# A nine-slot weight ring with three experts ahead of the loop, and token rows gathered by indirect DMA, in a two-layer trunk with a mixture of experts

## The chip, the cores and the metric

The kernel runs on one core of one Trainium2 chip, as one launch. The metric is the device time of one execution in microseconds, median of several runs. All data is float32.

## What is computed

Two residual layers over 512 tokens of width 1024 and a final RMSNorm. Layer 0 mixes with a gated linear recurrence beside chunked attention, layer 1 with a gated linear recurrence over eight heads. After each mixer comes a mixture of experts: 32 experts in 4 groups, each token takes the best group and the two best experts in it.

```python
def expert_block(args):
    toks, e = args
    xb = x_pad[toks]
    hb = jax.nn.silu(xb @ w_gate[e]) * (xb @ w_up[e])
    return hb @ w_down[e]
...
h = h + mix
h = h + hier_moe(rms_norm(h, norm_ffn_g[layer]), moe_router_group[layer], moe_router_expert[layer],
                 moe_w_gate[layer], moe_w_up[layer], moe_w_down[layer])
```

Each expert has a gate and an up matrix of 1024x512 and a down matrix of 512x1024, 2 MB each, so 6 MB per expert and 192 MB per layer. 1024 token rows (512 tokens, two experts each) are spread over the 32 experts: 32 rows on average, and the kernel gives each expert a block of CAP = 64.

## The kernel before, in words

Every engine has its own hand-written instruction stream; semaphores order them. `filled[b]` and `drained[b]` count uses of PSUM bank b: TensorE fills, VectorE or ScalarE drains. In the expert loop bank BX (0) holds the transposed token rows, BG (1) gate and up products in its two halves, BH (2) the transposed hidden rows, BY (3) the expert's output, BR (4) the picked token rows.

**Weights.** Two rings of three 2 MB slots, ring_a and ring_b. The mixers use ring_a; their scratch lies partly in ring_b. Experts alternate between the rings: slot 0 gate, slot 1 up, slot 2 down. SyncE issues all weight loads (`expert_load`, L395 to L402): gate and up of expert e+2 wait until the gate/up matmuls of expert e are done, down of e+2 until its down matmuls are. Expert 0 is loaded as soon as ring_b is free of the mixer's scratch, expert 1 only when the mixer's output projection (L490) is over; expert 2 is the first load of the loop.

**Routing.** `route` (VectorE, L1401) makes the one-hot choices, TensorE their running counts (bank "pos", L713 to L717). From these VectorE makes `slots` (L1459, L1461), for every token and expert the place in the expert's block, then the one-hot factors A and B (L1465 to L1469), from which TensorE makes a table of token numbers by place and expert (L726); VectorE turns it into the row numbers `ri` for the scatter (L1482 to L1487).

**Token rows.** For each expert VectorE compares a column of `slots` with a ramp (`select`, L1509): a 128x256 one-hot tile. `pick_rows` (L599) multiplies it with the normalised rows xh: 8 matmuls of 512 columns. ScalarE copies the picked rows out (`picked`, L922), `turn_picked` transposes them (L609), VectorE applies the gain (`turned`, L1521). POOL copies the column for `select` (L1106).

**One expert** on TensorE: `gate_up` (L622, 16 matmuls), `pick_rows` for e+2, `turn_hidden` (L628), `turn_picked` for e+1 (L609), `down` (L636, 8 matmuls). In the trace each float32 matmul stands as two instructions. Meanwhile ScalarE does the silu (L930) and half of the output copy (L936), VectorE the product (L1527), the copy of the hidden rows (L1540) and the other half of the output (L1548); POOL copies the expert's column of `ri` (L1118) and scatters the 64 output rows to DRAM by indirect DMA (L1093), rows without a token being skipped. PE's loop takes two experts per pass; the last two experts pick nothing.

**Around the loop.** After the last scatter ScalarE issues eight loads of the scattered rows (L973) into ring_b; VectorE combines them with h (L1593) and the next norm follows, in layer 1 the final norm (L1602), for which ScalarE has loaded `fin_g` ahead of its waits (L966). SyncE then loads the weights of the layer-1 mixer (L430 to L446): the second of them waits for the combined rows to have been read back. If an expert has more than 64 rows, `more_blocks` does the rest; this doesn't occur in the profiled execution.

## Time and profile before

| what | value |
|---|---|
| runs | 1745.91, 1752.74, 1749.08 us; median 1749.08 us |
| profiled execution, its own time | 1747.05 us |
| its span, first to last instruction | 1745.2 us |
| mean granted clock of TensorE | 0.970 |
| TensorE busy | 1634.0 us (94%) |
| VectorE, ScalarE, POOL busy | 526.9, 369.8, 223.2 us |
| moved by DMA | 463.23 MB, mean 265 GB/s |

All times of rows are microseconds from the span's start unless ns is written. A timeline row gives start, duration, engine, line, operation and tile, and in brackets the idle time before it with what ended it. In the rows of the windows view the PEclk column is the granted clock as a share of full speed. A DMA row ends with the median time from issue to landing. L12 is line 12 of the kernel.

### The profile page before, as it was taken

How to read it: one execution, taken by the hardware profiler on the slowest of the kernel's cores; microseconds unless marked ns; L12 is line 12 of the kernel's file. 1: busy time of each engine (PE TensorE's matmuls, PEld its weight loads, DVE VectorE, ACT ScalarE, POOL GpSimd, SP SyncE). 2: the span in 40 equal slices, each digit the busy share in tenths (PEclk: the TensorE clock that was granted, in tenths of full speed). 3: DMA queues.
4: the chain of work that ended last, by engine and by line, in shares of the span. 5: the costliest groups of instructions: out<-in, count | busy, mean ns of one | idle time of the engine just before them, and what ended most of it. 6: DMA issues, size and time to landing. Idle time of an engine off the chain costs nothing. (4 is left out here: it accounts for less than half of the span.)

```text
span 1745.2 us, 20175 instructions
## 1 busy us (share of the span) xinstructions
PE 1634.0 (94%) x7420; PEld 782.3 (45%) x7420; DVE 526.9 (30%) x1046; ACT 369.8 (21%) x599; POOL 223.2 (13%) x379
## 2 busy tenths in 40 slices
PE   7999997999999999994999999988899999999992
PEld 3444544444444444432577666645333333333330
DVE  4223534321221222224144444433322222222224
ACT  2032421111111111112344445421111111111111
POOL 2000000000000000000144444320000000000000
PEclk9999999999999999996999999999899999999997
DMA  6311033499999999996111112303399999999994
GB/s 217 99 49 54 25 151 145 181 427 429 428 426 428 427 430 428 428 388 245 49 49 49 49 52 99 140 1 145 151 423 428 428 429 429 428 428 428 428 413 168
DMA packets 53953, 463.23 MB, mean 265 GB/s; under 512 B 12800, under 2 KB 12808, under 8 KB 28304
## 3 DMA queue, kind: packets, MB, share of 16 engines
q1 hardware_dynamic: 46336, 445.26, 61.4%
q10 hardware_dynamic: 2448, 8.91, 1.3%
q0 software_dynamic: 5120, 8.40, 1.3%
q8 instruction: 31, 0.51, 0.1%
q14 instruction: 18, 0.15, 0.0%
HBM read 452.03 MB, written 18.89 MB: 270 GB/s over the span
## 5 line engine op out<-in xcount | busy, mean ns | idle before, releaser
L599 PE MATMUL ps<-sb_xh,sb_scr 128*64 128x512 f32 x1024 | 236.7, 602 | 2.4 <-DVE sb_scr L1509 2.4
L622 PE MATMUL ps<-sb_ring_a,sb_scr 128*64 128x512 f32 x1024 | 226.1, 592 | 0.0
L622 PE MATMUL ps<-sb_ring_b,sb_scr 128*64 128x512 f32 x1024 | 225.9, 592 | 0.0
L1527 DVE TENSOR_TENSOR sb_scr<-sb_scr,ps 64x512 f32<-64x512 f32 x64 | 67.6, 1055 | 394.1 <-ACT sb_scr L930 394.1
L755 PE MATMUL ps<-sb_xT,sb_ring_a 128*128 128x512 f32 x384 | 170.4, 598 | 1.1 <-DVE sb_xT L1251 1.1
L1093 POOL DMA_INDIRECT expert_rows<-sb_scr,sb_si x64 | 57.7, 902 | 875.6 <-DVE sb_scr L1548 875.6
L599 PEld LDWEIGHTS ps<-sb_xh,sb_scr 128*64 128x64 f32 x1024 | 86.2, 139 | 137.9 <-issue 137.9
L622 PEld LDWEIGHTS ps<-sb_ring_a,sb_scr 128*64 128x64 f32 x1024 | 88.5, 137 | 131.3 <-issue 131.3
L622 PEld LDWEIGHTS ps<-sb_ring_b,sb_scr 128*64 128x64 f32 x1024 | 83.3, 137 | 135.2 <-issue 135.2
L930 ACT ACTIVATE sb_scr<-ps 64x512 f32<-64x512 f32 x64 | 37.7, 590 | 401.8 <-PE ps L622 401.8
L636 PE MATMUL ps<-sb_ring_a,sb_scr 128*64 128x512 f32 x512 | 118.4, 604 | 1.1 <-issue 1.1
L636 PE MATMUL ps<-sb_ring_b,sb_scr 128*64 128x512 f32 x512 | 116.9, 597 | 0.0
L515 PE MATMUL ps<-sb_xT,sb_ring_a 128*128 128x512 f32 x256 | 110.3, 592 | 1.6 <-DVE sb_xT L1251 1.6
L755 PEld LDWEIGHTS ps<-sb_xT,sb_ring_a 128*128 128x128 f32 x384 | 72.0, 192 | 83.9 <-issue 83.9
L1548 DVE COPY sb_scr<-ps 64x512 f32<-64x512 f32 x64 | 44.4, 693 | 214.0 <-ACT sb_scr L936 214.0
L922 ACT ACTIVATE sb_scr<-ps 128x512 f32<-128x512 f32 x64 | 38.2, 597 | 251.9 <-PE ps L609 226.9
L936 ACT ACTIVATE sb_scr<-ps 64x512 f32<-64x512 f32 x64 | 37.9, 592 | 207.7 <-PE ps L636 207.7
L515 PEld LDWEIGHTS ps<-sb_xT,sb_ring_a 128*128 128x128 f32 x256 | 48.6, 190 | 62.6 <-issue 62.6
L1665 DVE COPY_PREDICATED sb_scr<-sb_masks,ps 128x512 f32<-128x512 uint32 x56 | 40.9, 731 | 104.8 <-PE ps L770 104.8
L770 PEld LDWEIGHTS ps<-sb_scr 128*128 128x128 f32 x512 | 61.2, 192 | 9.1 <-issue 9.1
L636 PEld LDWEIGHTS ps<-sb_ring_b,sb_scr 128*64 128x64 f32 x512 | 40.4, 136 | 55.1 <-issue 55.1
L1540 DVE COPY sb_scr<-ps 128x256 f32<-128x256 f32 x64 | 27.2, 425 | 125.3 <-PE ps L628 125.3
(230 smaller groups left out, 1626.0 us busy)
## 6 DMA issues: line engine op xcount, KB each, us to landing
sb_ring_b<-in_w_gate_dram SPq DMA_DIRECT2D x32, 2048.0 KB
sb_ring_b<-in_w_up_dram SPq DMA_DIRECT2D x32, 2048.0 KB, 17.2
sb_ring_b<-in_w_down_dram SPq DMA_DIRECT2D x32, 2048.0 KB, 14.8
sb_ring_a<-in_w_gate_dram SPq DMA_DIRECT2D x32, 2048.0 KB
sb_ring_a<-in_w_up_dram SPq DMA_DIRECT2D x32, 2048.0 KB, 17.3
sb_ring_a<-in_w_down_dram SPq DMA_DIRECT2D x32, 2048.0 KB, 15.0
sb_ring_a<-in_c_w_in_dram SPq DMA_DIRECT2D x8, 2048.0 KB, 7.8
sb_ring_a<-in_ab_w_in_dram SPq DMA_DIRECT2D x5, 2048.0 KB, 11.3
```

The lines of the kernel that those rows point to most:

```text
L515: mm = nc.tensor.matmul(dst[:], a, b, start=(c == 0), stop=(c == NC - 1))
L599: mm = nc.tensor.matmul(ps[BR][64 * z:64 * z + CAP, :], me["sel"][:, j, t * CAP:(t + 1) * CAP], xh[:, t, z * 512:(z + 1) * 512], start=(t ...
L622: mm = nc.tensor.matmul(ps[BG][64 * s:64 * s + CAP, :], me["xgT"][:, j, c * CAP:(c + 1) * CAP], wblock(r, s, NC)[:, c, :], start=(c == 0), ...
L636: mm = nc.tensor.matmul(ps[BY][64 * z:64 * z + CAP, :], me["hT"][:, c * CAP:(c + 1) * CAP], wblock(r, 2, FC)[:, c, z * 512:(z + 1) * 512], ...
L755: mm = nc.tensor.matmul(dst[:], w[:, c, k, :], xT[:, c, :], start=(c == 0), stop=(c == NC - 1))
L770: mm = nc.tensor.matmul(dst[:, sl], a[:, sl], b[:, sl], start=True, stop=True)
L922: A(me["picked"], ps[BR][:], ACT.Copy).then_inc(drained[BR], 1)
L936: A(me["rows"][0:CAP, 2 + j, 0:512], ps[BY][0:CAP, :], ACT.Copy).then_inc(half_out, 1)
L1093: g.indirect_dma_start(out=y_d[l], out_offset=bass.IndirectOffsetOnAxis(ap=si[j][:, 0:1], axis=0), in_=me["rows"][0:CAP, 2 + j, :], in_off ...
L1527: return v.tensor_tensor(me["hrow"][0:CAP, :].rearrange("p (c q) -> p q c", c=FC), by_q(me["silu"][64:128, j, :]), by_q(ps[BG][64:128, :]) ...
L1548: v.tensor_copy(me["rows"][0:CAP, 2 + j, 512:1024], ps[BY][64:128, :]).then_inc(drained[BY], 1)
L1665: drains(v.copy_predicated(dst, masks[:, L - 1, :].bitcast(U32).unsqueeze(1).broadcast_to([P, NT, P]), src), job)
```

## The change

It does three things. (1) The six slots of the two rings become one ring of nine; an expert's three matrices go to slots by expert number modulo 3. The room comes from `xh` (it is now slot 8) and from the scratch, part of which now lies in slots 6 and 7. Experts 0 to 2 are loaded ahead of the loop: expert 1 without the wait for the output projection, expert 2's gate and up as the projection frees slots 2 and 0, its down when xh has been transposed and stored. In layer 1 expert 0 is loaded during the mixer. Loads of expert e+3 wait for expert e. (2) The normalised rows are stored to DRAM (ScalarE issues four DMAs) and POOL gathers the 64 rows of an expert with an indirect DMA, two experts ahead; eight transposes of 64x128 (`turn_in`) bring them to BX. `select`, `pick_rows`, `picked`, `turn_picked`, `slots` and bank BR go. The table is completed (one more column of steps, and `xi`) before the first gather. (3) PE's loop takes six experts per pass, the load of `fin_g` is issued after the last scatter's wait, and the second and third weight load of the layer-1 mixer no longer wait for the rows read back.

```diff
+SLOTS, SLOT = 9, 8 * 512
+EXPERT_SLOTS = ((3, 4, 5), (6, 7, 1), (2, 0, 8))
...
+        yrows = slots(3, 2).rearrange("p (a d) -> p a d", d=D)
...
+            def weight_load(l, e, q, part):
+
+                w, s = (w_gate, w_up, w_down)[part], EXPERT_SLOTS[q][part]
+                sp.dma_start(ring[:, s, :], by_partition(w[l, bass.ds(e, 1)])).then_inc(ring_in[s], 16)
+
+            def expert_load(l, e, q):
+
+                sp.wait_ge(filled[BG], e + (moe_base[l][BG] - 2))
+                weight_load(l, e, q, 0)
+                weight_load(l, e, q, 1)
+                sp.wait_ge(filled[BY], e + (moe_base[l][BY] - 2))
+                weight_load(l, e, q, 2)
...
+                else:
+                    wait_full(sp, ("c", HEADS_C - 1, 3))
+                    sp.wait_ge(y_ready, HEADS_C)
+                if l == 0:
+                    for part in range(3):
+                        weight_load(l, 0, 0, part)
+                for part in range(3):
+                    weight_load(l, 1, 1, part)
+                for part in range(2):
+                    wait_full(sp, ("out", l, NT - 1, part))
+                    weight_load(l, 2, 2, part)
+                wait_full(sp, ("xt", 2 * l + 1, NT - 1, 1))
+                sp.wait_ge(xh_stored[l], 16 * NT)
+                weight_load(l, 2, 2, 2)
+                with sp.Fori(1, NE // 3) as i:
+                    for q in range(3):
+                        expert_load(l, i * 3 + q, q)
...
-            sp.wait_ge(filled[BG], moe_base[0][BG] + NE)
+            sp.wait_ge(filled[BG], moe_base[0][BG] + NE - 2)
...
                 if i == 1:
-                    sp.wait_ge(yrow_in[NT - 1], 32)
-                if i == 2:
                     sp.wait_ge(filled[BY], moe_base[0][BY] + NE)
...
+                if i == 3:
+                    sp.wait_ge(h_ready, 2 * NT)
+                    for part in range(3):
+                        weight_load(1, 0, 0, part)
...
-                if ahead >= 2:
-                    pick_rows(l, e + 2, j)
+                gate_up(three, q % 2).then_inc(filled[BG], 1)
+                if not last:
+                    turn_gathered(l, e + 1, i * 3 + (q + 1) // 2, (q + 1) % 2)
                 pe.wait_ge(drained[BG], e + (base[BG] + 1))
...
-                if ahead >= 1:
-                    turn_picked(l, e + 1)
...
-                pick_rows(l, 0, 0)
-                turn_picked(l, 0)
-                pick_rows(l, 1, 1)
...
+                turn_gathered(l, 0, 0, 0)
+                for e in range(6):
+                    expert(l, e, 0, e)
+                with pe.Fori(1, NE // 6) as i:
+                    for q in range(6):
+                        expert(l, i * 6 + q, i, q)
...
                 norm(2 * l + 1)
+                for t in range(NT):
+                    act.wait_ge(xh_ready, (2 * l + 1) * NT + t + 1)
+                    act.dma_start(xg_d[l][t * P:(t + 1) * P, :], xh[:, t, :]).then_inc(xh_stored[l], 16)
...
+            def gather_rows(l, j):
+                pool.sem_inc(moving, 1)
+                g.indirect_dma_start(out=me["gat"][0:CAP, j, :], out_offset=None, in_=xg_d[l],
+                                     in_offset=bass.IndirectOffsetOnAxis(ap=gi[j][:, 0:1], axis=0),
+                                     bounds_check=T - 1, oob_is_err=False).then_inc(gathered[j], 16)
...
                     if ahead:
-                        pool.wait_ge(sel_ready, e + (l * NE + 2))
-                        slots_of(e + 3, 1 - j)
+                        pool.wait_ge(filled[BX], e + (base[BX] + 1))
+                        fetch(e + 2, j)
...
+                    if ahead:
+                        pool.wait_ge(idx_copied, e * 2 + (2 * l * NE + 4))
+                        gather_rows(l, j)
...
+                st.then(v.tensor_scalar(tab[:, 2, :], tab[:, 0, :], T + 0.5, -float(T), ALU.is_gt, ALU.mult))
+                v.tensor_copy(ri[:], tab[:, 1, :])
+                v.tensor_tensor(xi[:], tab[:, 1, :], tab[:, 2, :], ALU.add).then_inc(table_ready, 1)
+                turned(l, 0, 0)
```

## Rows read from the trace of the kernel before

**Rows 1.** The page: bytes moved, in 40 slices of the span.
```profile
GB/s 217 99 49 54 25 151 145 181 427 429 428 426 428 427 430 428 428 388 245 49 49 49 49 52 99 140 1 145 151 423 428 428 429 429 428 428 428 428 413 168
```

**Rows 2.** Windows, in the loop of layer 1 (columns: page's engines, PEclk, DMA share, GB/s).
```profile
1400.00:1500.00 100.00, 100.00 (x488) 38.93 (x488) 21.35 (x34) 11.87 (x20) 8.53 (x21) 1.00 1.01 428
```

**Rows 3.** Timeline of TensorE, one expert of the loop in layer 0.
```profile
499.68 7.07 PE L622 MATMUL ps<-sb_ring_b,sb_scr 128*64 128x512 f32 x32
506.54 3.63 PE L599 MATMUL ps<-sb_xh,sb_scr 128*64 128x512 f32 x16
510.50 0.66 PE L609 MATMUL ps<-sb_ident,sb_scr 128*128 128x128 f32 x4
511.13 3.65 PE L636 MATMUL ps<-sb_ring_b,sb_scr 128*64 128x512 f32 x16
514.59 7.07 PE L622 MATMUL ps<-sb_ring_a,sb_scr 128*64 128x512 f32 x32
```

**Rows 4.** DMA issues, up matrix: experts 2, 31 of layer 0, then of layer 1.
```profile
sb_ring_b<-in_w_up_dram SPq DMA_DIRECT2D x1, 2048.0 KB, 13.3
...
sb_ring_a<-in_w_up_dram SPq DMA_DIRECT2D x1, 2048.0 KB, 19.3
...
sb_ring_b<-in_w_up_dram SPq DMA_DIRECT2D x1, 2048.0 KB, 12.1
...
sb_ring_a<-in_w_up_dram SPq DMA_DIRECT2D x1, 2048.0 KB, 20.2
```

**Rows 5.** The page, DMA queues: packets, MB, share; this is all 64 scatters.
```profile
q0 software_dynamic: 5120, 8.40, 1.3%
```

**Rows 6.** Timeline of TensorE, experts 30 and 31; last row layer 1.
```profile
768.03 7.07 PE L622 MATMUL ps<-sb_ring_b,sb_scr 128*64 128x512 f32 x32
...
781.36 7.07 PE L622 MATMUL ps<-sb_ring_a,sb_scr 128*64 128x512 f32 x32
...
791.25 5.09 PE L636 MATMUL ps<-sb_ring_a,sb_scr 128*64 128x512 f32 x16 [0.56 <-issue]
...
1710.60 3.65 PE L636 MATMUL ps<-sb_ring_a,sb_scr 128*64 128x512 f32 x16 [0.56 <-issue]
```

**Rows 7.** Timeline, from the normalised rows to the loop; last two rows layer 1.
```profile
287.55 1.33 DVE L1240 TENSOR_SCALAR sb_xh<-sb_h,sb_rstd 128x1024 f32<-128x1024 f32 x1
...
308.82 0.29 DVE L1459 SCALAR_TENSOR_TENSOR sb_scr<-ps,sb_scr 128x128 f32<-128x128 f32 x1 [1.29 <-PE ps L717]
...
309.98 5.09 PE L599 MATMUL ps<-sb_xh,sb_scr 128*64 128x512 f32 x16 [1.20 <-DVE sb_scr L1509]
310.08 0.28 DVE L1465 TENSOR_TENSOR sb_scr<-ps,sb_scr 128x128 f32<-128x128 f32 x1
...
312.48 0.42 DVE L1469 TENSOR_TENSOR sb_scr<-sb_iota,sb_scr 128x256 f32<-128x256 f32 x1
...
320.79 7.06 PE L622 MATMUL ps<-sb_ring_b,sb_scr 128*64 128x512 f32 x31
...
320.99 0.18 DVE L1482 COPY sb_scr<-ps 64x32 f32<-64x32 f32 x1 [3.79 <-PE ps L726]
...
321.63 0.17 DVE L1487 CAST sb_ri<-sb_scr 64x32 uint32<-64x32 f32 x1
...
1228.43 6.66 PE L599 MATMUL ps<-sb_xh,sb_scr 128*64 128x512 f32 x16 [1.20 <-DVE sb_scr L1509]
...
1240.81 7.06 PE L622 MATMUL ps<-sb_ring_b,sb_scr 128*64 128x512 f32 x31
```

**Rows 8.** The scatter's line L1093, all 64 of them.
```profile
DMA to landing us min/median/max: 2.5/7.9/8.7
```

**Rows 9.** Timeline, from the last scatter of layer 0 to the read back.
```profile
798.54 0.89 POOL L1093 DMA_INDIRECT expert_rows<-sb_scr,sb_si  x1 [13.68 <-DVE sb_scr L1548]
802.30 4.80 ACTq L973 DMA_DIRECT2D sb_ring_b<-expert_rows  x8
```

**Rows 10.** Windows, at the end of layer 0's loop.
```profile
788.00:792.00 4.00, 1.61 (x9) 0.64 (x8) 1.45 (x2) 0.59 (x1) 0.00 (x0) 0.85 0.68 197
```

More of the change, by code:

```diff
@@ new lines, in trunk @@
+        m1.update(carve(high, [("f", (T,)), ("eb", (T,)), ("qe", (2, T)), ("dl", (3, P)), ("kh", (3, P)),
+                               ("st", (2, 3 * P)), ("sq", (T,)), ("rs", (T,))]))
+        m1.update(carve(slots(8, 1), [("y", (8, T))]))
+        me = carve(low, [("gat", (2, D)), ("rows", (2, D))])
+        me.update(carve(high, [("xgT", (2, NC * CAP)), ("hT", (FC * CAP,)), ("silu", (F,)),
+                               ("hrow", (F,)), ("lg", (NT, NG + NE)), ("em", (NT, NE)), ("key", (NT, NE)),
+                               ("M0", (NT, NE)), ("M1", (NT, NE)), ("M", (NT, NE)), ("pos", (2, NT)),
+                               ("A", (2, NT, CAP)), ("B", (2, NT, NE)), ("g4", (NT, NG)), ("goh", (NT, NG)),
+                               ("ex", (NT, 5)), ("tab", (3, NE)), ("w", (12, NT)), ("lgT", (T,)), ("Msum", (NT, NE))]))
@@ L174, in trunk @@
+        me.update(carve(high, [("fin_g", (D,))]))
+        yrows = slots(3, 2).rearrange("p (a d) -> p a d", d=D)
         filled = [sem(f"filled{b}") for b in range(8)]
         drained = [sem(f"drained{b}") for b in range(8)]
-        ring_in = {(r, s): sem(f"ring_in_{r}{s}") for r in "ab" for s in range(3)}
+        ring_in = [sem(f"ring_in{s}") for s in range(SLOTS)]
         x_in = [sem(f"x_in{t}") for t in range(NT)]
@@ L213, in trunk @@
         xh_stored = [sem(f"xh_stored{l}") for l in range(2)]
-        col_ready, sel_ready = sem("col_ready"), sem("sel_ready")
+        gathered = [sem(f"gathered{j}") for j in range(2)]
         scattered = [sem(f"scattered{j}") for j in range(2)]
@@ L246, in plan_moe @@
             moe_base.append(list(bk.uses))
-            for b in (BX, BG, BH, BY, BR):
+            for b in (BX, BG, BH, BY):
                 bk.uses[b] += NE
@@ L407, in moe_loads @@
                     wait_full(sp, ("O", NA - 1))
-                expert_load(l, 0, 0, True)
-                for nb in range(2):
-                    wait_full(sp, ("out", l, NT - 1, nb))
-                expert_load(l, 1, 1, True)
-                with sp.Fori(0, NE // 2 - 1) as i:
-                    expert_load(l, i * 2 + 2, 0, False)
-                    expert_load(l, i * 2 + 3, 1, False)
+                else:
[15 more added lines that the diff above has]
+                        expert_load(l, i * 3 + q, q)
+                for e in range(NE // 3 * 3, NE):
+                    expert_load(l, e, e % 3)
             def more_loads(l):
@@ L630, in turn_hidden, with down @@
                 return mm
-            def down(r):
+            def down(slots):
                 for c in range(FC):
@@ L728, in moe @@
                 fills(mm, ("tab", l))
-                expert(l, 0, 0, 0)
-                with pe.Fori(0, NE // 2 - 2) as i:
-                    expert(l, i * 2 + 1, i, 1)
-                    expert(l, i * 2 + 2, i + 1, 0)
-                expert(l, NE - 3, NE // 2 - 2, 1)
-                expert(l, NE - 2, NE // 2 - 1, 0, ahead=1)
-                expert(l, NE - 1, NE // 2 - 1, 1, ahead=0)
+                turn_gathered(l, 0, 0, 0)
[4 more added lines that the diff above has]
+                        expert(l, i * 6 + q, i, q)
+                for e in range(NE // 6 * 6, NE):
+                    expert(l, e, NE // 6, e % 6, last=e == NE - 1)
                 more_blocks(l)
@@ L1457, in route @@
                 wait_full(dve, job)
-                st.then(v.scalar_tensor_tensor(out=me["slots"], in0=bank(job)[:, 0:NT * NE].rearrange(
-                    "p (t n) -> p t n", t=NT), scalar=1.0, in1=M, op0=ALU.add, op1=ALU.mult))
-                st.then(v.tensor_scalar(me["slots"], me["slots"], -1.0, None, ALU.add))
-                for e in range(2):
-                    select(l, e, e)
                 for k, Mk in ((0, M0), (1, M1)):
```

290 lines of the change are left out of this document (111 added, 179 removed).

## The prediction

> **What bounds the kernel now.** First I read the bytes by slices [rows 1]: twice there are about ten slices at 427 to 430 GB/s, the expert loops, and between them long stretches at 50 to 150. The windows view of such a stretch [rows 2] shows DMA at a share of 1.01 and TensorE busy for 100 of 100 us: both are full, and the question is which of them sets the pace. The timeline [rows 3] says TensorE: experts follow each other at 514.59 - 499.68 = 14.91 us without a gap, gate/up 6.86, picking 3.6, turns about 1.0, down 3.46. The landings [rows 4] say how near DMA is. Loads are issued at TensorE's pace, yet issue to landing of the up matrix grows from 13.3 to 19.3 us over 29 experts in layer 0 and from 12.1 to 20.2 in layer 1: 0.21 and 0.28 us each. So DMA's own pace is 15.12 to 15.19, I take **15.15 us per expert**, and it is slower than TensorE; only the lead from two preloaded experts hides it. TensorE's loop can get faster by its lead only: what counts is how many bytes are left to move once the loop starts, and at what rate.
>
> **The change, part by part.**
>
> *Picking goes, turning comes.* Per expert 3.6 us of matmuls [rows 3] leave TensorE, and the turn of picked rows (0.66). Eight transposes of gathered rows come, about 0.9 us (estimate from the four of L609). They don't add: the last experts of layer 0 already run without picking [rows 6], at 781.36 - 768.03 = 13.33 us, and there TensorE waits between gate/up and down for silu and product (788.43 to 791.25, 2.82 us); the transposes fall into that wait. So TensorE needs **13.34 us per expert**, 1.8 below DMA. DMA becomes the bound.
>
> *Gathers on the DMA engines.* The same 16 engines now also read the token rows. All 64 scatters, 8.40 MB, took 1.3% of the engines' span, so 22.7 us or 0.355 us each [rows 5]; a gather moves the same rows the other way, so I take 0.35 and DMA's pace becomes **15.50 us**. Bounds: below, nothing (reads might fit beside the writes, though a share of 1.01 speaks against it); above, 0.71, if the empty half of the 64 places or an uneven spread over the engines costs as much again. I take the scatter's row, as it is the nearest.
>
> *Three experts ahead.* 29 instead of 30 experts remain for the loop. Expert 2 fits into the idle time before it: the output projections and the routing lie there, and the slices stand at 145 GB/s [rows 1]. The four stores of the normalised rows (2 MB, 5 us at 428 GB/s) start behind the last norm step at 287.55 + 1.33 and are needed only when the table is done, past 314: hidden by the routing. Expert 0 of layer 1 goes into the mixer's stretch at 49 to 99 GB/s: hidden.
>
> *Sum for the loop.* Up of expert 3 lands 0.7 us (issue of gate ahead of it, estimate) plus 12.1 to 13.3 [rows 4], so 13.4 us, after gate/up of expert 0. Up of expert 31 lands 28 x 15.50 = 434.0 us later, then gate/up 7.07, wait 2.82, down 3.65: the loop ends 461.0 us after gate/up of expert 0. Before it was 796.34 - 327.85 = 468.5 in layer 0 and 1714.25 - 1247.87 = 466.4 in layer 1 [rows 6, 7]. Gain 7.5 and 5.4 us. Early in the loop TensorE works off the lead and no load waits for it: at 13.34 against 15.50 it is out of lead near expert 14.
>
> *Start of the loop.* Now the first expert needs the table. From the running counts at 308.82 [rows 7]: `slots` and two selections go (310.08 - 308.82 = 1.26 saved), so the factors are ready at 312.90 - 1.26 = 311.64; table matmuls 1.0 to 2 us, take 1.5; the table steps 0.81 and two more at 0.21 each, with the wake-up 1.35; table ready near 314.5. POOL then copies an index (0.3) and gathers. For the gather of an idle queue the scatter gives 2.5 us from issue to landing, and up to 3.76 from the last scatter's issue to the read back [rows 8, 9]: take 3.1, so 318. Turning 1.2, gain 0.85, and gate/up starts near 320.1, where it started at 320.79. But picking no longer warms TensorE up. The first picks took 5.09 and 6.66 us where the later ones took 3.63 [rows 3, 7], so 1.5 to 3.0 us go onto gate/up now: take 2.2. It ends 1.5 us later than before in layer 0, and by the same steps 0 us later in layer 1, whose picks had been colder. Bounds -3 to +5 us per layer.
> By the Trainium skill (DMA: Bandwidth & Descriptors, Anatomy of one DMA) a DMA issued by POOL takes about 2.0 us plus its bytes at 436 GB/s, an estimate of 2.3 us here; by that the start would come 0.8 us earlier per layer than by the row I use.
>
> *Between the layers.* Two mixer loads of 2 MB (9.8 us at 428 GB/s) are now issued right behind the last down matmuls, ahead of the last scatter and the read back. In an idle queue the scatter was done in 3.76 us [rows 9]; in a full one it lands after 7.9 [rows 8]. So the read back comes 0 to 6 us later, take 3.5. Nothing is won by the earlier loads, as the mixer's first weights are there anyway. POOL: its gather stands ahead of the scatter of expert e and behind that of e-1, and it has a period and a half to land in; 7.9 us fits.
>
> *At the end.* `fin_g` is issued ahead of the eight read-backs, 0.6 us by their 4.80 for eight [rows 9], and 0.5 MB of transfer: +1.2 us.
>
> *Total.* Layer 0: -7.5 + 1.5 + 3.5 = -2.5; layer 1: -5.4 + 0 + 1.2 = -4.2. Together **-6.7 us** on a profiled execution of 1747.05 (span 1745.2). The median of the runs shown is 2.0 us above it, so the forecast is 1749.08 - 6.7, about **1742 us**. This case has its own range of 1733 to 1752.
>
> **The rivals.**
>
> (a) *The gathers cost DMA nothing.* Then 57 x 0.35 = 20 us more are won: 1722. For it speaks that scatters write to DRAM and gathers read from it; against it the share of 1.01, as weight loads are reads too. Chance 0.08.
>
> (b) *A gather costs twice the scatter's share* (0.71 each): 20 us more, 1762, slower than before. It decides from 0.47 us per gather on, where the 6.7 us are eaten. For it: 5120 packets are 80 for each 64 places, half of which are empty (8.40 MB are 2050 rows of 4 KB), and the engine with most rows sets the landing. Chance 0.15.
>
> (c) *The clock.* TensorE will wait for weights in every expert (15.50 - 13.34 = 2.2 us) besides the waits around the turns. In layer 0's last expert, which had such waits, the granted clock fell to 0.85 of full speed over four microseconds, so to its lower level of 1.2 GHz for part of it, and down took 5.09 instead of 3.65 [rows 6, 10]; in layer 1 the same expert kept the full 2.4 GHz level. One such fall costs 1.4 to 3.0 us of TensorE; it decides where more than 2.2 us per expert are lost. At 3.0 each time it would be 57 x 0.8 = 46 us: 1788, and with half the experts about 1765. It checks itself: a TensorE that has become the bound no longer waits for weights. Chance 0.12.
> The Trainium skill (TensorE: Matmul & The Clock Gate, HAM oscillation) says that a DMA wait before each group of matmuls throws the engine back to 1.2 GHz every time, which speaks against this change; this trace agrees in one of two last experts.
>
> (d) *The third expert isn't ahead.* Its down waits for the stores and the transposes; if anything of it slips behind the loop's start, the lead is two and a part, up to 15.5 us lost per layer: 1773 at worst. For it speaks only the chain of waits in SyncE; the idle slices speak against. Chance 0.04.
>
> **How the numbers follow.** The main case has 0.61. A measurement of this kernel tells about 0.5%, 8.7 us, from no change, and the forecast lies at -7: of the main case 0.43 is faster by more, 0.55 within, 0.02 slower. Faster: 0.26 + 0.08 from (a) = 0.34, rounded to 0.35. Slower: (b) mostly, (c), (d) and a little of the main case, 0.30. Within: 0.35. The range of 1722 to 1772 takes in (a), (b), (d) but for its end, and the milder half of (c); it leaves out about 0.15.
>
> **What would show it.** In the profile of the changed kernel: DMA at a share of 1.0 through both loops, and a TensorE that waits about 2 us before gate/up from the middle of each loop on, its busy share there below 90%. Issue to landing of up near 38 us late in the loop, and experts following at 15.4 to 15.6 us: more says (b) when TensorE waits for DMA, (c) when it doesn't and L622 takes over 7.07. The software queue should hold 2 x 8.4 MB at 2.6%. First gate/up at 320 in layer 0; the gather behind the table landing in 2.5 to 3.8 us. Read back of layer 0 about 9 us behind the last down matmuls, where it was 6. The forecast is wrong if the period is under 15.2 or over 15.9, or if the loop is still paced by TensorE.

## The result, and the profile after

The changed kernel takes 1796.69 us (median of 4 runs, 1793.12 to 1797.92), the kernel before 1748.99 us beside it. The ratio is 1.0268, 95% interval 1.0243 to 1.0293: 47.7 us slower, where 1742 us with a range up to 1772 was forecast. The profiled executions have spans of 1791.1 and 1745.2 us; the trace below has to explain 45.9 us.

The page of the changed kernel: TensorE's busy line, the bytes by slices, the two main queues, and the two gate/up and turn groups.

```profile
PE 1474.3 (82%) x6652; PEld 710.0 (40%) x6652; DVE 502.7 (28%) x982; ACT 331.9 (19%) x535; POOL 287.0 (16%) x447
...
GB/s 211 96 47 53 30 255 214 257 397 408 414 409 410 411 411 401 405 384 195 134 102 48 48 94 48 1 188 141 244 405 399 406 412 412 414 405 408 411 342 159
...
q1 hardware_dynamic: 46336, 445.26, 61.9%
q0 software_dynamic: 10240, 16.80, 2.8%
...
L616 PE MATMUL ps<-sb_ring,sb_work 128*64 128x512 f32 x2048 | 471.2, 613 | 71.8 <-DMA sb_ring<-in_w_up_dram 59.4
...
L622 PE MATMUL ps<-sb_ident,sb_work 64*128 64x64 f32 x256 | 27.6, 228 | 83.4 <-DVE sb_work L1498 83.4
...
sb_ring<-in_w_up_dram SPq DMA_DIRECT2D x64, 2048.0 KB, 39.5
```

The slices are the news. Where the kernel before moved 426 to 430 GB/s in nearly all full slices of its loops [rows 1], this one moves 397 to 414, though it has the gathered rows to move besides the weights. The queue of the indirect DMAs, q0, doubled its bytes, as forecast, and has a share of 2.8%, where 2.6% was forecast from [rows 5]. TensorE now waits 59.4 us in all for the up matrix.

Windows of the changed kernel: the stretch of [rows 2], then the whole of each loop (us, busy time and count of PE, PEld, DVE, ACT, POOL, then PEclk, DMA share, GB/s).

```profile
1400.00:1500.00 100.00, 76.25 (x370) 28.69 (x368) 17.69 (x25) 7.68 (x13) 13.84 (x25) 0.96 1.01 410
...
330.00:800.00 470.00, 373.95 (x1828) 146.98 (x1828) 87.09 (x123) 35.96 (x61) 64.52 (x118) 0.96 1.00 407
1272.00:1740.00 468.00, 379.25 (x1811) 146.06 (x1812) 87.11 (x123) 35.47 (x61) 64.55 (x118) 0.94 1.00 405
```

The DMA share is 1.00 to 1.01 as before, so the engines are as occupied, but 5% fewer bytes pass. The timeline of TensorE in the middle of layer 0's loop answers to [rows 3]:

```profile
603.64 7.09 PE L616 MATMUL ps<-sb_ring,sb_work 128*64 128x512 f32 x32 [0.68 <-DMA sb_ring<-in_w_up_dram]
610.65 0.71 PE L608 MATMUL ps<-sb_ident,sb_work 64*128 64x64 f32 x8
612.55 0.43 PE L622 MATMUL ps<-sb_ident,sb_work 64*128 64x64 f32 x4 [1.19 <-DVE sb_work L1498]
613.55 3.65 PE L630 MATMUL ps<-sb_ring,sb_work 128*64 128x512 f32 x16 [0.56 <-issue]
620.01 7.09 PE L616 MATMUL ps<-sb_ring,sb_work 128*64 128x512 f32 x32 [2.82 <-DMA sb_ring<-in_w_up_dram]
```

One expert takes 620.01 - 603.64 = 16.37 us. TensorE is through with it at 613.55 + 3.65 = 617.20, so after 13.56 us, and the wait of 2.82 us ahead of the next gate/up is for the up matrix, so for the DMA.

The start of both loops and the end of layer 0, on the timeline, answer to [rows 7, 9] (in the second part the read back is split by the listing, the row shows six of its eight issues):

```profile
313.67 0.18 DVE L1474 TENSOR_TENSOR sb_xi<-sb_work 64x32 uint32<-64x32 f32 x1
...
315.08 1.14 POOL L1083 DMA_INDIRECT sb_work<-norm_rows,sb_gi  x1 [0.99 <-POOL sb_gi L1094]
...
318.77 1.09 PE L608 MATMUL ps<-sb_ident,sb_work 64*128 64x64 f32 x8 [6.08 <-DMA sb_work<-norm_rows,sb_gi]
...
320.64 9.22 PE L616 MATMUL ps<-sb_ring,sb_work 128*64 128x512 f32 x32 [0.78 <-DVE sb_work L1485]
...
815.17 0.80 SPq L453 DMA_DIRECT2D sb_ring<-in_c_w_in_dram  x2
...
817.34 0.90 POOL L1077 DMA_INDIRECT expert_rows<-sb_work,sb_si  x1 [13.63 <-DVE sb_work L1517]
826.88 3.73 ACTq L957 DMA_DIRECT2D sb_ring<-expert_rows  x6
...
1261.60 9.77 PE L616 MATMUL ps<-sb_ring,sb_work 128*64 128x512 f32 x32 [0.78 <-DVE sb_work L1485]
```

The first gate/up starts at 320.64 and takes 9.22 us, where a later one takes 7.09: TensorE had waited for the gather, and in the trace its granted clock is 0.5, the lower of its two levels, until 325.0. In layer 1 the first takes 9.77, with the lower level until 1267.1. Below, such a start is called cold. From the scatter to the read back pass 9.54 us where 3.76 passed before.

Laid side by side (us; "loop" is from the start of the first gate/up to the end of the last down matmul):

| part | before | after | difference |
|---|---|---|---|
| to the first gate/up of layer 0 | 320.7 | 320.6 | 0 |
| loop of layer 0 | 475.7 | 494.5 | +18.8 |
| from it to the first gate/up of layer 1 | 444.4 | 446.4 | +2.0 |
| loop of layer 1 | 473.6 | 494.9 | +21.3 |
| from it to the end | 30.9 | 34.6 | +3.7 |

All but 6 us lies in the loops. The weights' packets say in what form: the trace records each of the 16 KB packets of the weight queue. Worked out from these records, in layer 0 from 420 to 700 us:

```
kernel before     mean 0.614 us
changed kernel    mean 0.639 us, 5% of them 0.818 or more
```

The slow ones, of 0.7 us or more, come in one group for each gather, most of them 2.4 to 3.4 us long and the longest 5.1, with up to 16 slow packets at once, as many as there are DMA engines. Weight packets that overlap only a gather's rows took 0.760 us on average; those beside a scatter's rows in the kernel before took 0.613. So the scatters' rows don't do this.

The rows' own packets are the smaller part. The share of q0 is 2.8% of 1791.1 us, or 50.2 us, and the scatters took 22.7 of it before [rows 5]: 27.5 us for 64 gathers, 0.43 us each.

### The profile page after: what moved, and what is told of

The parts are those of the page before. It is cut to its first block and busy times, and to the rows that moved or that the text cites. A ratio compares the mean times of both kernels' runs of the same rounds, so it can differ in the third digit from the quotient of the medians.

```text
span 1791.1 us, 18344 instructions
## 1 busy us (share of the span) xinstructions
PE 1474.3 (82%) x6652; PEld 710.0 (40%) x6652; DVE 502.7 (28%) x982; ACT 331.9 (19%) x535; POOL 287.0 (16%) x447
## 5 line engine op out<-in xcount | busy, mean ns | idle before, releaser
L616 PE MATMUL ps<-sb_ring,sb_work 128*64 128x512 f32 x2048 | 471.2, 613 | 71.8 <-DMA sb_ring<-in_w_up_dram 59.4
L616 PEld LDWEIGHTS ps<-sb_ring,sb_work 128*64 128x64 f32 x2048 | 164.6, 141 | 372.9 <-issue 337.3
L630 PE MATMUL ps<-sb_ring,sb_work 128*64 128x512 f32 x1024 | 265.9, 666 | 35.9 <-issue 33.8
L1498 DVE TENSOR_TENSOR sb_work<-sb_work,ps 64x512 f32<-64x512 f32 x64 | 65.4, 1023 | 493.6 <-ACT sb_work L919 493.6
L1077 POOL DMA_INDIRECT expert_rows<-sb_work,sb_si x64 | 58.8, 919 | 810.5 <-DVE sb_work L1517 810.5
L752 PE MATMUL ps<-sb_work,sb_ring 128*128 128x512 f32 x384 | 168.5, 592 | 1.1 <-DVE sb_work L1242 1.1
L630 PEld LDWEIGHTS ps<-sb_ring,sb_work 128*64 128x64 f32 x1024 | 88.5, 152 | 165.3 <-issue 162.7
L919 ACT ACTIVATE sb_work<-ps 64x512 f32<-64x512 f32 x64 | 37.8, 590 | 524.8 <-PE ps L616 524.8
L923 ACT ACTIVATE sb_work<-ps 64x512 f32<-64x512 f32 x64 | 37.9, 592 | 414.6 <-PE ps L630 414.6
L530 PE MATMUL ps<-sb_work,sb_ring 128*128 128x512 f32 x256 | 110.3, 592 | 1.6 <-DVE sb_work L1242 1.6
L752 PEld LDWEIGHTS ps<-sb_work,sb_ring 128*128 128x128 f32 x384 | 71.3, 190 | 82.6 <-issue 82.6
L530 PEld LDWEIGHTS ps<-sb_work,sb_ring 128*128 128x128 f32 x256 | 48.6, 190 | 62.6 <-issue 62.6
L1083 POOL DMA_INDIRECT sb_work<-norm_rows,sb_gi x64 | 61.3, 958 | 54.5 <-POOL sb_si L1105 48.3
L767 PEld LDWEIGHTS ps<-sb_ring 128*128 128x128 f32 x512 | 61.2, 192 | 9.1 <-issue 9.1
L767 PE MATMUL ps<-sb_ring 128*128 128x128 f32 x512 | 62.4, 275 | 0.0
## 6 DMA issues: line engine op xcount, KB each, us to landing
sb_ring<-in_w_gate_dram SPq DMA_DIRECT2D x64, 2048.0 KB, 34.6
```

The source lines that it names most:

```text
L530: mm = nc.tensor.matmul(dst[:], a, b, start=(c == 0), stop=(c == NC - 1))
L616: mm = nc.tensor.matmul(ps[BG][64 * z:64 * z + CAP, :], me["xgT"][:, j, c * CAP:(c + 1) * CAP], wblock(slots[z], NC)[:, c, :], start=(c == ...
L630: mm = nc.tensor.matmul(ps[BY][64 * z:64 * z + CAP, :], me["hT"][:, c * CAP:(c + 1) * CAP], wblock(slots[2], FC)[:, c, z * 512:(z + 1) * 512],
L752: mm = nc.tensor.matmul(dst[:], w[:, c, k, :], xT[:, c, :], start=(c == 0), stop=(c == NC - 1))
L767: mm = nc.tensor.matmul(dst[:, sl], a[:, sl], b[:, sl], start=True, stop=True)
L1077: g.indirect_dma_start(out=y_d[l], out_offset=bass.IndirectOffsetOnAxis(ap=si[j][:, 0:1], axis=0), in_=me["rows"][0:CAP, j, :], in_offset= ...
```

## The experiments

The theory: something about the gather makes the weights beside it slower. The rivals: nine slots in flight do it by themselves; the falls of TensorE's clock do it.

**1. No gathers in the loop**, and three kernels in which a plain DMA of 32 fixed rows on the same queue stands for the gather. These, and the other kernels with a plain copy below, leave out the choice of rows. Where a kernel writes partitions above 63, it also clears the whole buffer ahead of the loop; this edit isn't shown.

```diff
 # e1_none
-                        gather_rows(l, j)
-                pe.wait_ge(gathered[j], k * 16 + 16 * (l * (NE // 2) + 1))
+                pe.wait_ge(gathered[j], 16 * (l + 1))
 # e2_plain, in place of the indirect gather
+                g.dma_start(me["gat"][0:32, j, :], xg_d[l][0:32, :]).then_inc(gathered[j], 16)
 # e3_spread
+                g.dma_start(me["gat"][:, j, 0:256], xg_d[l][0:32, :].rearrange("r (q n) -> (r q) n", q=4)
+                            ).then_inc(gathered[j], 16)
 # e4_dram
+                g.dma_start(dump[j], xg_d[l][0:32, :]).then_inc(gathered[j], 16)
```

> This kernel leaves out the gathers of experts 2 to 31 of each layer: those experts compute on the rows gathered for experts 0 and 1. Everything else of the changed kernel stays (nine slots, three experts ahead, the scatters, the copies of the indices). Theory G (the gather costs the DMA engines about 1.0 us per expert: 0.4 for its own rows and 0.6 because the weight packets beside it take 0.64 us in place of 0.61): the late experts of both loops come down from 16.25 to 16.5 us each to about 15.2, mean weight packets to 0.61 us, and with 29 experts in each layer the time is 1797 - 58 x 1.0 = 1738 us. Rival D (the deeper backlog of loads makes the weight packets slower by itself): packets stay at 0.64 us, only the rows' own 0.4 us goes, about 1773 us. Rival C (the falls of TensorE's clock, not the DMA, set the pace): the falls of 3.4 us stay and the time stays within 8 us of 1797.

> This kernel leaves out the choice of rows: in place of each indirect gather it copies the first 32 rows of the layer's normed tokens, in one plain DMA on the same queue, to the first 32 partitions. Same bytes, about the same rows per packet, same partitions written; no dummies and no scattered reads. Theory P (the place written, a few partitions, is what slows the weights' packets): still 1790 to 1800 us. Rival I (indirection or the scattered reads do it): 1740 to 1765 us, weight packets at 0.61 us.

> As the kernel with the plain copy, the same 32 rows and 128 KB, but written as 1 KB pieces over all 128 partitions. Theory P (few partitions are the cause): 1750 to 1770 us, with weight packets back at about 0.61 us and only the bytes' own time left. Rival I or rival H (reading the rows from DRAM is the cost, wherever they go): no more than 5 us from the plain copy to 32 partitions.

> As the kernel with the plain copy, but the 32 rows go to a scratch in DRAM and not to the SBUF; TensorE turns rows that stay zero. It leaves out the rows altogether and keeps their reads, the queue, and the bytes. Theory P (the write into the SBUF is what slows the weights): 1745 to 1765 us, weight packets about 0.61 us. Rival H (the read from DRAM beside the weights' reads is the cost): as slow as the plain copy to 32 partitions or slower, near 1790 us.

Measured: without gathers 1725.23 us (ratio to before 0.9866, interval 0.9845 to 0.9887). Plain copy to partitions 0 to 31: 1781.65 us (1.0190, 1.0172 to 1.0209). The same bytes over all partitions: 1744.03 us (0.9971, 0.9959 to 0.9984). From DRAM to DRAM: 1742.65 us (0.9968, 0.9954 to 0.9982). All four came out below the ranges that were expected of the theory; e2_plain lies between its two theories' ranges, nearer to the first. The windows view, 1400 to 1500 us, of the four in this order:

```profile
1400.00:1500.00 100.00, 85.48 (x428) 33.78 (x426) 20.51 (x29) 8.28 (x15) 8.41 (x21) 0.97 1.01 429
```
```profile
1400.00:1500.00 100.00, 81.04 (x380) 30.53 (x378) 16.98 (x24) 7.08 (x12) 12.49 (x28) 0.93 1.01 409
```
```profile
1400.00:1500.00 100.00, 83.74 (x408) 32.18 (x404) 19.13 (x27) 7.67 (x13) 12.42 (x28) 0.95 1.01 426
```
```profile
1400.00:1500.00 100.00, 83.83 (x410) 32.33 (x408) 19.81 (x28) 8.26 (x14) 12.60 (x28) 0.95 1.01 428
```

429, 409, 426, 428 GB/s. A backlog of nine slots costs nothing: e1_none has it at 429. Indirection and scattered reads aren't the main cost, since a plain copy of 32 neighbouring rows moves as few bytes as the gather (409 against 410). They, or something else that the plain copy leaves out, may hold a part of the 15 us by which e2_plain is faster than the changed kernel; 6.8 us of these lie in the two loops. Reading the rows isn't the cost either, since the copy to DRAM reads them as well. It is the write into partitions 0 to 31.

Without gathers the experts follow each other at the pace of the weights alone, in layer 0 of e1_none (755.56 - 664.61) / 6 = 15.16 us:

```profile
664.61 7.09 PE L616 MATMUL ps<-sb_ring,sb_work 128*64 128x512 f32 x32 [1.62 <-DMA sb_ring<-in_w_up_dram]
...
755.56 7.09 PE L616 MATMUL ps<-sb_ring,sb_work 128*64 128x512 f32 x32 [1.78 <-DMA sb_ring<-in_w_up_dram]
```

Its loops took 460.5 and 460.0 us, which prices everything that follows: a gather costs (loop - 460.5 or 460.0) / 29, as 29 experts' weights are loaded in a loop. For the changed kernel that is **1.17 and 1.20 us**, where the forecast had 0.35.

**2. Which partitions?** Three more plain copies and, in c1_half, the real rows, gathered as half rows by 128 indices.

```diff
 # e7_every4
+                g.dma_start(me["gat"][0:P:4, j, :], xg_d[l][0:32, :]).then_inc(gathered[j], 16)
 # e8_half2
+                g.dma_start(me["gat"][0:P:2, j, 0:512], xg_d[l][0:32, :].rearrange("r (q n) -> (r q) n", q=2)
+                            ).then_inc(gathered[j], 16)
 # e5_sbuf
+                g.dma_start(me["gat"][0:32, j, :], me["gat"][32:64, j, :]).then_inc(gathered[j], 16)
 # c1_half; the table is made for both halves, an index is 2 * token + half
+                g.indirect_dma_start(out=me["gat"][:, j, 0:512], out_offset=None,
+                                     in_=xg_d[l].rearrange("t (z n) -> (t z) n", z=2),
...
```

> Plain copy of 32 whole rows (4 KB each) as in the kernel that took 1781.65 us, but to every fourth partition (0, 4, ... 124) in place of partitions 0 to 31. It leaves out the choice of rows. The copy in 1 KB pieces to all partitions took 1744.03 us. Theory N (what slows the weights is that the rows' destinations are neighbours, and so share the same ports into the SBUF): within 6 us of 1744. Rival L (what slows them is that a whole 4 KB row goes to one partition, wherever that lies): within 6 us of 1782.

> Plain copy of the same 32 rows as 64 half rows of 2 KB to every second partition. It leaves out the choice of rows. Theory N: within 6 us of 1744, since the destinations lie over the whole SBUF. Rival L: about halfway, 1755 to 1770 us.

> Plain copy of 32 rows of 4 KB from partitions 32 to 63 of the SBUF to partitions 0 to 31: nothing is read from DRAM. It leaves out the rows altogether. If the write to neighbouring partitions is all of the extra price: 1775 to 1790 us, as the copy from DRAM (1781.65). If the DRAM read has a part in it: less, 1745 to 1770 us. If reading neighbouring partitions costs as much as writing them: above 1800 us.

> The changed kernel with the right rows, but gathered by 128 indices as half rows of 2 KB: the first halves to partitions 0 to 63, the second halves to partitions 64 to 127 (an expert's rows fill the first half of each), turned by four transposes of 128 x 128 in place of eight of 64 rows. Theory N: the conflict is over twice as many partitions, so the extra of 38 us (1781.65 - 1744.03) is halved or better: 1750 to 1775 us. Rival I (that part of the changed kernel's 1797 us which the plain copy to the same partitions does not have, 15 us, is the price of indirection, and doubles with twice the indices): 1785 us or more.

Measured: 1740.21 us (every fourth partition), 1740.86 (half rows, every second), 1779.80 (from the SBUF, nothing read from DRAM), 1755.61 us with the right rows (c1_half; ratio to before 1.0037, 1.0024 to 1.0050). All four lie in the ranges expected of theory N. Rival L falls: a whole row may go to one partition. The copy within the SBUF settles that the write alone is slow, and that reading 32 neighbouring partitions beside it adds nothing. And c1_half is the first version with the real rows near the old time.

**3. The same with the real rows.** An expert's rows fill the first places of its block of 64, so renumbering the places moves them. c2_iota does only this to the changed kernel, c3_spread to c1_half. c4_both also restores the old wait ahead of the second mixer load.

```diff
-            g.iota(iota[:], [[1, CAP]], base=0,
+            g.iota(iota[:], [[1, CAP // 2], [CAP // 2, 2]], base=0,
...
 # c4_both, in the loads of the layer-1 mixer, i == 1
                     sp.wait_ge(filled[BY], moe_base[0][BY] + NE)
+                    sp.wait_ge(yrow_in[NT - 1], 32)
```

> The changed kernel with one line changed: the places of an expert's 64 slots are numbered 0, 32, 1, 33, ..., so that its first 32 rows (nearly all that it has) are gathered to partitions 0, 2, ... 62 in place of 0 to 31. Same rows, bytes, packets and instructions. Theory N (neighbouring destinations share ports): as with half rows to two halves of the SBUF, twice as many places: 1750 to 1770 us. Rival (only the number of instructions and descriptors of the indirect gather counts): 1790 to 1800 us.

> The kernel with half rows on 128 indices (1755.61 us) with the same renumbering of the slots: the 64 half rows of an expert go to every second partition, as in the plain copy that took 1740.86 us. Theory N: 1737 to 1747 us, the whole extra price gone, weight packets at 0.617 us or less. Rival I (indirection itself costs what is left between 1740.86 and 1755.61): 1750 us or more.

> The kernel with the spread half rows, and the second weight load of the next layer's mixer waits for the read back of the expert rows, as it did in the kernel before. Theory B (the three weight loads that now go out ahead of the last scatter and the read back delay these by some 6 us): 3 to 6 us less than the kernel with the spread half rows alone. Rival (those loads are needed by the first projections, and then start them later): within 2 us of it, or slower.

Measured: c2_iota 1789.02 us, a miss for theory N (1750 to 1770): rows on 0, 2, ... 62 are hardly faster than on 0 to 31. c3_spread 1746.66 us (0.9986, 0.9977 to 0.9995): 50 us of the changed kernel's time are gone. It differs from that kernel by half rows, 128 indices and other transposes as well; the plain copies of whole rows, e2_plain and e7_every4, differ by the partitions alone (and the clearing), and they are 41 us apart. c4_both 1742.53 us (0.9963, 0.9949 to 0.9977), 4.1 us less again. The windows view of c2_iota, then of c3_spread:

```profile
1400.00:1500.00 100.00, 78.80 (x376) 29.36 (x374) 17.69 (x25) 7.68 (x13) 13.11 (x24) 0.95 1.01 408
```
```profile
1400.00:1500.00 100.00, 82.26 (x382) 30.91 (x380) 19.83 (x28) 8.26 (x14) 14.40 (x26) 0.97 1.01 426
```

c2_iota (32 places among 0 to 62: 408 GB/s) against c1_half (0 to 31 and 64 to 95: 426) says that neighbours are not the point, and points to the halves of the SBUF. On the wait, the timeline of c3_spread and then of c4_both:

```profile
794.01 0.80 SPq L454 DMA_DIRECT2D sb_ring<-in_c_w_in_dram  x2
796.18 0.91 POOL L1083 DMA_INDIRECT expert_rows<-sb_work,sb_si  x1 [12.11 <-DVE sb_work L1530]
805.96 3.85 ACTq L963 DMA_DIRECT2D sb_ring<-expert_rows  x8
```
```profile
792.37 0.91 POOL L1084 DMA_INDIRECT expert_rows<-sb_work,sb_si  x1 [12.11 <-DVE sb_work L1531]
796.16 3.86 ACTq L964 DMA_DIRECT2D sb_ring<-expert_rows  x8
...
808.90 0.80 SPq L455 DMA_DIRECT2D sb_ring<-in_c_w_in_dram  x2
```

Two mixer loads ahead of the scatter make it land 9.78 us behind its issue, and 3.79 us without them. The stretch between the loops shrank from 447.2 to 440.5 us.

**4. One half or neighbours, tested alone.**

```diff
 # f1_twohalves
+                for z in range(2):
+                    g.dma_start(me["gat"][64 * z:64 * z + 16, j, :], xg_d[l][16 * z:16 * z + 16, :]
+                                ).then_inc(gathered[j], 16)
 # f2_lower
+                g.dma_start(me["gat"][0:64:2, j, :], xg_d[l][0:32, :]).then_inc(gathered[j], 16)
 # g1_upper
+                g.dma_start(me["gat"][64:P:2, j, :], xg_d[l][0:32, :]).then_inc(gathered[j], 16)
```

> Plain copy of 32 whole rows in two DMAs of 16 rows, to partitions 0 to 15 and 64 to 79; it leaves out the choice of rows. Theory S (the two halves of the SBUF, partitions 0 to 63 and 64 to 127, have paths of their own, and rows that all go to one half are what slows the weights' packets): 1738 to 1750 us and weight packets of 0.61 to 0.62 us, though the destinations are neighbours. Rival N (neighbouring destinations, in whichever half): 1765 us or more.

> Plain copy of 32 whole rows in one DMA to partitions 0, 2, ... 62; it leaves out the choice of rows. Theory S: as slow as the copy to partitions 0 to 31 (1781.65 us), within 8 us, since all rows go to the lower half. Rival N: about halfway to the kernel with every fourth partition (1740.21), 1755 to 1765 us or less.

> Plain copy of 32 whole rows in one DMA to partitions 64, 66, ... 126; it leaves out the choice of rows. Theory S, mended after the run with two DMAs (rows slow the weights' packets while all rows in flight at one time go to one half of the SBUF; of those two DMAs one follows the other): as slow as the copy to 0, 2, ... 62 (1781.93 us), within 8 us. Rival L (only the lower partitions are slow): within 6 us of 1740. Rival M (what counts is the number of partitions in any half): the same forecast as S, so it is not told apart here.

Measured: 1781.93 us for 0, 2, ... 62 and 1785.69 for 64, 66, ... 126, both as theory S has it, so the one half is as slow as the other when all rows go to it. But 1809.84 us for 0 to 15 and 64 to 79, the slowest of all placements, at 399 GB/s:

```profile
1400.00:1500.00 100.00, 78.49 (x368) 29.34 (x364) 17.00 (x24) 7.08 (x12) 13.55 (x30) 0.93 1.01 399
```

For this run theory S, as it was put, fails: both halves were written, and it was slow. Its two DMAs follow each other: in the trace their rows stand in two bursts of 16, for one expert from 522.6 and from 524.4 us. So at any one time the rows go to 16 neighbouring partitions of one half. That it is this, and not having two DMAs for each expert, which makes it the slowest wasn't tried alone; what the second DMA adds to the queue's records are 1024 packets of 4 bytes. Together the placements give this table (each price is worked out from the two loops as above; packets are the means of the weight queue's 16 KB packets, 420 to 700 us):

| kernel | partitions that an expert's rows reach | price of one gather or copy, us | weight packet, us |
|---|---|---|---|
| e1_none | no gathers | 0 (it sets the zero) | 0.614 |
| e4_dram | none | 0.28, 0.32 | 0.614 |
| e7_every4 | 0, 4, ... 124 | 0.31, 0.30 | 0.614 |
| e8_half2 | 0, 2, ... 126 | 0.38, 0.32 | 0.615 |
| e3_spread | all | 0.38, 0.39 | 0.617 |
| c3_spread | 0, 2, ... 126 | 0.32, 0.37 | 0.616 |
| c1_half | 0 to 31, 64 to 95 | 0.49, 0.52 | 0.616 |
| e5_sbuf | 0 to 31 | 0.97, 1.00 | 0.640 |
| f2_lower | 0, 2, ... 62 | 1.03, 1.02 | 0.642 |
| g1_upper | 64, 66, ... 126 | 1.11, 1.00 | 0.644 |
| e2_plain | 0 to 31 | 1.08, 1.06 | 0.641 |
| c2_iota | 0, 2, ... 62 | 1.01, 1.10 | 0.641 |
| changed kernel | 0 to 31 | 1.17, 1.20 | 0.639 |
| f1_twohalves | 0 to 15, then 64 to 79 | 1.42, 1.58 | 0.655 |

The Trainium skill (SBUF — State Buffer, Door 1: The DMA port swizzle) has a rule that fits every line: bits 4 to 2 and bit 6 of the partition number choose one of 16 ports for the DMA side, so that partitions 0 to 63 reach eight of them and adding 32 changes nothing. By it the rows that cost 0.3 to 0.5 us reach all 16 ports (or none), those at about 1.0 to 1.2 reach eight, and f1_twohalves four at a time. The runs agree in order and grouping; they don't show the ports themselves.

Left open is why c1_half costs 0.15 us more than c3_spread per gather and the changed kernel 0.1 more than c2_iota. In c1_half more packets of the queue carry only empty places (598 packets of 8 bytes from 420 to 700 us, against 117 in c3_spread), so some engines may have more rows than others; this wasn't tried alone. It can't be told of the other pair, whose packets have the same sizes and numbers.

**5. TensorE's clock.** In the loops of c4_both the granted clock falls to its lower level for a while in 10 of each loop's groups of gate/up or down matmuls, besides the cold first one, as it does in 12 and 15 of them in the changed kernel; the kernel before kept 1.00 up to the last expert [rows 2, 10]. The fillers are matmuls on constants into the bank that picking no longer uses.

```diff
+            def fill(n):
+                for _ in range(n):
+                    nc.tensor.matmul(ps[4][0:CAP, :], ones[:, 0:CAP], keep[:], start=True, stop=True)
 # c5_fill: 8 behind down.  f3_fill: 1 behind turn_gathered, 2 behind down.
 # f4_warm: 3 ahead of the turn of expert 0.  g2_fill: those 3, then 1 behind turn_gathered, 1 behind down.
```

> The kernel with the spread half rows and the wait, and eight matmuls of 512 columns per expert on constants into an unused bank, issued behind the down projection: what TensorE did for picking before, about 1.6 us. They fill its waits for the weights. Theory F (the DMA sets the pace, and the falls of the clock cost only where TensorE ends last): granted clock up to 0.96 or more, time within 4 us of the kernel without them. Rival C (the falls of the clock are paid in the time): 10 us or more faster. Rival (the filled stretches make TensorE the bound again): slower by 5 us or more.

> The kernel with the spread half rows and the wait (1742.53 us), and three matmuls of 512 columns per expert on constants into an unused bank: one where TensorE waits for the activation (1.3 us idle there) and two behind the down projection, 0.88 us each. TensorE then needs about 13.34 + 1.8 = 15.1 us per expert, under the DMA's 15.5. Theory F (the DMA sets the pace; the falls of the clock are paid at the ends of the loops only): granted clock up from 0.946 to 0.97 or more, time within 5 us of 1742.5. Rival C (the falls are paid all along): 10 us or more faster. Rival (the filling takes back what was gained): over 5 us slower.

> The kernel with the spread half rows and the wait, and three matmuls on constants in the 6 us in which TensorE waits for the first gather of each layer. In the profile of the kernel without them the first gate and up projection takes 9.3 us, at half clock in part, against 7.1 later. Theory W (it starts slow because TensorE stood idle before it, and the loop's end moves with its start): about 2 us less in each layer, 1736 to 1741 us. Rival (the DMA sets the loop's end whatever the first expert takes): within 1.5 us of 1742.5.

> The fastest kernel so far (1735.54 us: spread half rows, the wait, three matmuls on constants ahead of the first expert) and per expert two such matmuls, one in the wait for the activation and one behind the down projection. With three, TensorE needed 15.2 us per expert in the trace and was the bound over all 32 experts (32 x 15.2 = 486 against the DMA's 468 for 29). With two it needs about 14.3 us, 32 x 14.3 = 458, under the DMA's 468. Theory F (the falls of the clock are no part of the time where the DMA sets the pace): 1732 to 1738 us, with the clock at full speed in the loops. Rival C (the falls are paid): 1730 us or less. Rival (any filling is paid): 1745 us or more.

c5_fill took 2106.65 us. I had sized the filler by the 3.6 us that picking took for as many instructions, but picking wrote its two output halves in turn; here the eight matmuls, all into one half, take about 7 us. f3_fill, sized by the mean of one, still lost: 1772.89 us (1.0133), where at most 5 us more than c4_both's 1742.53 were expected. Its timeline shows an expert of 523.73 - 508.42 = 15.31 us:

```profile
508.42 7.40 PE L622 MATMUL ps<-sb_ring,sb_work 128*64 128x512 f32 x31
515.76 0.66 PE L647 MATMUL ps<-sb_ident,sb_work 128*128 128x128 f32 x4
516.34 1.07 PE L616 MATMUL ps<-sb_keep,sb_ones 128*64 128x512 f32 x2
517.94 0.43 PE L628 MATMUL ps<-sb_ident,sb_work 64*128 64x64 f32 x4 [0.52 <-DVE sb_work L1518]
518.93 3.65 PE L636 MATMUL ps<-sb_ring,sb_work 128*64 128x512 f32 x16 [0.56 <-issue]
...
523.73 7.40 PE L622 MATMUL ps<-sb_ring,sb_work 128*64 128x512 f32 x31
```

That is below the DMA's 15.5 and yet too much, as the two don't count the same experts: TensorE does 32 of them (this one took 15.31, the next 15.05; 32 x 15.2 = 486, the loops took 485.2 and 485.3), the DMA moves 29. The point where they are equal is 470 / 32 = 14.7 us.

f4_warm took **1735.54 us** (0.9926, 0.9912 to 0.9939; 1736 to 1741 expected), g2_fill 1734.26 (0.9921, 0.9908 to 0.9935). Timeline of c4_both's first gate/up, then f4_warm's:

```profile
320.02 9.31 PE L618 MATMUL ps<-sb_ring,sb_work 128*64 128x512 f32 x32 [0.78 <-DVE sb_work L1506]
```
```profile
321.20 7.09 PE L622 MATMUL ps<-sb_ring,sb_work 128*64 128x512 f32 x32 [0.78 <-DVE sb_work L1511]
```

Its first gate/up is as fast as the later ones from the start, and the loops end 2.2 and 2.6 us sooner after their start. That is 4.8 us of the 7.0 between the medians; the runs of c4_both alone lie 8 us apart, so the rest isn't told from that spread. Windows of the loops of f4_warm, then of g2_fill:

```profile
330.00:780.00 450.00, 376.36 (x1722) 145.83 (x1724) 86.81 (x124) 35.95 (x61) 67.56 (x120) 0.96 1.01 425
1250.00:1690.00 440.00, 366.45 (x1678) 140.14 (x1676) 84.96 (x120) 35.35 (x60) 65.69 (x116) 0.96 1.00 424
```
```profile
330.00:780.00 450.00, 412.09 (x1842) 156.08 (x1842) 88.03 (x124) 36.38 (x62) 67.56 (x120) 1.00 1.01 425
1250.00:1690.00 440.00, 403.34 (x1800) 150.94 (x1799) 85.19 (x120) 35.35 (x60) 66.71 (x119) 1.00 1.01 425
```

With the granted clock at 1.00 throughout, g2_fill's loops take 467.9 and 467.9 us, and f4_warm's, at 0.96, 467.9 and 467.9. The falls inside a loop that the DMA paces cost nothing. The cold first expert cost its 2.2 and 2.6 us, as the loads of the loop wait for the first gate/up to be done. In the changed kernel itself this wasn't tried.

## Why the prediction was wrong

- **The step that failed** is "Gathers on the DMA engines": "a gather moves the same rows the other way, so I take 0.35", with an upper bound of 0.71. The scatter's row [rows 5] priced the bytes, and for the bytes it was right: 0.28 to 0.39 us where the rows are spread evenly over both halves or stay in DRAM. It could not price the other direction. A scatter reads partitions 0 to 31, a gather writes them, and the write costs 1.17 to 1.20 us, over the bound, because the weights' own packets slow down meanwhile: 0.760 us beside its rows where 0.614 is the mean without gathers. That is a cost to other transfers, and the prediction had no term for it. The excess of 0.83 us on 58 gathers is 48 us, and the loops missed their forecast by just that: 461.0 us plus a first gate/up of 9.22 and 9.77 gives 470.2 and 470.8, measured 494.5 and 494.9, so 24.3 and 24.1 us more. That is 48.4 of the 52.6 us between the forecast difference of -6.7 and the 45.9 of the profiles.
- **DMA's pace without gathers** was right: 15.16 us in e1_none, forecast 15.15. So was the sum of the loop with a gather at 0.35: c3_spread's loops are 469.9 and 470.6 us. (The slices from which it starts run from 426 GB/s, not 427; nothing hangs on that.)
- **TensorE at 13.34 us** and the change of bound were right: early experts with the full clock start 349.56 - 336.22 = 13.34 us apart, later it waits for the up matrix.
- **The start** was right within 1 us: table at 313.85 (314.5), turn at 318.77 (318), gate/up 320.64 (320.1), 2.2 and 2.7 us cold (2.2). In part that is luck: the experiments with the same instructions ahead of the first gather, such as e1_none and c2_iota, have this gate/up up to 4.6 us later in their profiles (325.23, 324.85). And two terms were off in opposite ways: the matmuls for the table started 0.9 us sooner and took 1.92 us, for which 1.5 stood there without a row. The first gather landed 3.56 us (layer 1: 3.06) behind its issue, for 3.1 taken; the other estimate given there, 2.3, was short.
- **Between the layers** the mechanism was right and the size was at its end: the scatter took 5.8 us longer to the read back (3.5, bounds 0 to 6). c3_spread against c4_both shows 6.7 us for it in the profile, 4.1 in the medians. The stretch as a whole grew by 2.0 only, since from the read back to the first gate/up of layer 1 pass 434.7 us where 438.4 passed before; 2.2 us less was forecast of that. **The end** cost 3.7 us, not 1.2: scatter to read back 4.80 us for 3.99, 0.40 of which is the issue of `fin_g` in between, and the first combination 7.9 us behind the read back's issue for 4.9. Why this last is longer wasn't tested.
- **Rival (b)** named the right term with the wrong reason and too small a price; empty places and uneven engines can explain at most 0.1 to 0.15 us of it. Its 1762 would have needed 0.71.
- **Rival (c)**: behind the first expert the clock fell 12 and 15 times in the two loops, not in every expert; the Trainium skill's rule (TensorE: Matmul & The Clock Gate, HAM oscillation), by which each wait for a DMA sends the engine back, agrees with part of them. Behind the first expert it cost nothing where tested (g2_fill against f4_warm), since the engine had the time; in the changed kernel itself the sign is that TensorE still waits for the DMA.
- **Rivals (a) and (d)** fall: gathers cost something wherever they go, and the third expert was ahead, as its gate/up began without a wait.
- What the text itself named as telling signs did tell: the period of 16.37, over its 15.9, with TensorE waiting for the DMA said (b), not (c). The sign that it had not named is the one that showed the cause: a DMA share of 1.0 with fewer GB/s.

## What to carry to other kernels

A transfer has a price of its own and a price for what runs beside it; where the DMA engines are full, ask which partitions a small transfer writes, not only how many bytes. Here 128 KB cost 1.2 us on partitions 0 to 31 and 0.35 when every second partition of the whole SBUF took half a row; half rows by 128 indices, a renumbered table of places, a wait put back and three matmuls on constants ahead of the first expert made a version 0.74% faster than the kernel before (f4_warm). And when two engines race through a loop with a lead, count each one's experts: TensorE's 32 against the DMA's 29.

## What the runs showed of the hardware that was not expected

- A write of 128 KB into partitions of one half of the SBUF lengthens the weight queue's 16 KB packets from 0.613 us up to 0.82 and more, and the 16 engines still show a share of 1.00 to 1.01. Reading partitions for the scatters leaves them at 0.613.
- How slow it is depends on which partitions are written at one time. It isn't neighbourhood (c1_half has neighbours at 0.5 us, f2_lower has none at 1.0), nor the number of partitions or the bytes in each (e7_every4, 32 whole rows, 0.3 us, as many as in f2_lower).
- A cold first gate/up of 9.3 and 9.7 us (c4_both) takes 7.09 us when matmuls on constants, 4.35 and 4.15 us of them, run ahead of it (f4_warm), in time in which TensorE waited anyway.
